# Two spatial gating layers: every projection from seven block products in place of eight

## The reference, cut to what matters

```python
def sgu_mixer(h, w_in, gain, w_s, b_s, w_out):
    u, v, z = jnp.split(h @ w_in, 3, axis=-1)          # 1024 -> 3 x 2048
    u = jax.nn.gelu(u)
    v = rms_norm_2(jax.nn.gelu(v), gain)
    vc = v.reshape(bsz, length // 128, 128, 8, 256)
    mixed = jnp.einsum('gpq,bcqgd->bcpgd', w_s, vc) + b_s.T[:, :, None]
    s = u * mixed.reshape(bsz, length, 2048)
    return (s * jax.nn.silu(z)) @ w_out                # 2048 -> 1024
```

## Time and profile before

| | |
|---|---|
| runs, median (lowest to highest) | 4984.64 us (4980.01 to 4988.49) |
| span of the profiled execution | 4981.9 us |
| TensorE busy | 4775.0 us, 96% |
| VectorE, ScalarE, GpSimd busy | 1474.1, 1080.2, 322.4 us |
| layer 0: v, u and z with mixing, out | from 1789.89, 1956.08 and 2311.37 us |
| layer 3: u and z with mixing, out | from 4623.95 and 4860.86 us |

### The profile page before, as it was taken

How to read it: one execution, slowest core, us unless ns; L and a number is a source line. 1 busy time by engine, 2 the same in 40 slices (tenths; PEclk the granted TensorE clock), 3 DMA queues, 4 the chain that set the end, 5 groups by cost and what they waited for, 6 DMA issues and landing times.

```text
span 4981.9 us, 62040 instructions
## 1 busy us (share of the span) xinstructions
PE 4775.0 (96%) x26926; PEld 2606.3 (52%) x26926; DVE 1474.1 (30%) x2789; ACT 1080.2 (22%) x2094; POOL 322.4 (6%) x302
## 2 busy tenths in 40 slices
PE   8999999999999999999999988988999999999999
PEld 4444444444444444665545557776544555644443
DVE  3621110363111010000044337785301443410100
ACT  1131000113100022110033124443211333311210
POOL 1100000110000000000003200000000101000000
PEclk9999999998999999999999999999999999999999
DMA  3151212115122211111134332322111000111211
GB/s 122 60 203 68 76 67 77 70 59 203 61 78 70 71 50 68 51 43 50 54 127 137 128 91 79 82 78 105 60 50 52 28 14 28 44 51 68 84 68 59
DMA packets 115069, 378.31 MB, mean 76 GB/s; under 512 B 32752, under 2 KB 58480, under 8 KB 85360
## 3 DMA queue, kind: packets, MB, share of 16 engines
q1 hardware_dynamic: 103840, 332.92, 19.2%
q0 software_dynamic: 9808, 37.75, 2.3%
q10 hardware_dynamic: 1152, 3.67, 0.2%
HBM read 334.46 MB, written 39.85 MB: 75 GB/s over the span
## 4 chain that ended last, share of the span: by engine, by line
PE 90%; DVE 6%; ACT 2%; issue 2%; DMA 0%; POOL 0%; POOLq 0%; DVEq 0%; ACTq 0%; SPq 0%
PE ps L522 43%; PE ps L334 21%; PE ps L543 7%; PE ps L3421 2%; PE ps L1782 2%; PE ps L340 2%; PE ps L3343 1%; PE ps L991 1%; PE ps L947 1%; PE ps L3432 1%; PE ps L2437 1%; PE ps L3346 1%; PE ps L3342 1%; PE ps L3344 1%; PE ps L450 0%
## 5 line engine op out<-in xcount | busy, mean ns | idle before, releaser
L522 PE MATMUL ps<-A,W 128*128 128x512 f32 (+1 forms) x5344 | 2149.8, 562 | 23.6 <-DVE A L494 8.8
L522 PEld LDWEIGHTS ps<-A,W 128*128 128x128 f32 x5344 | 1017.5, 192 | 1105.4 <-issue 1063.1
L334 PE MATMUL ps<-A,W 64*64 64x64 f32 (+3 forms) x3264 | 661.7, 380 | 10.1 <-ACT A L3586 5.8
L334 PEld LDWEIGHTS ps<-A,W 128*128 128x128 f32 (+2 forms) x3264 | 349.8, 163 | 305.8 <-issue 282.1
L334 PEld LDWEIGHTS ps<-A 64*64 64x64 f32 (+2 forms) x8416 | 401.1, 147 | 150.1 <-issue 94.9
L334 PE MATMUL ps<-A 64*64 64x64 f32 (+3 forms) x8416 | 438.2, 237 | 42.9 <-ACT A L2653 14.1
L543 PE MATMUL ps<-W,A 128*128 128x512 f32 (+1 forms) x896 | 366.0, 570 | 1.8 <-ACT A L1568 1.8
L543 PEld LDWEIGHTS ps<-W,A 128*128 128x128 f32 x896 | 172.0, 193 | 191.1 <-issue 183.8
L436 ACT ACTIVATE A<-R 128x512 f32<-128x512 f32 (+1 forms) x96 | 52.6, 574 | 759.3 <-DVE R L1578 330.5
L1698 DVE SCALAR_TENSOR_TENSOR A<-ps,V,A 128x512 f32<-128x512 f32 (+1 forms) x48 | 31.0, 661 | 486.9 <-PE ps L334 486.3
L1578 DVE SCALAR_TENSOR_TENSOR R<-ps,MOD,R 128x512 f32<-128x512 f32 (+1 forms) x48 | 31.7, 662 | 416.7 <-PE ps L522 410.6
(11 more groups left out here) (360 smaller groups left out, 4202.8 us busy)
## 6 DMA issues: line engine op xcount, KB each, us to landing
W<-in_ada SPq DMA_DIRECT2D x48, 1024.0 KB, 5.4
W<-in_w_up SPq DMA_DIRECT2D x44, 1024.0 KB, 4.8
W<-in_w_down SPq DMA_DIRECT2D x32, 704.0 KB, 4.1
W<-in_w_in SPq DMA_DIRECT2D x18, 1024.0 KB, 4.8
W<-in_sgu_v SPq DMA_DIRECT2D x16, 1024.0 KB, 4.9
W<-in_sgu_u SPq DMA_DIRECT2D x16, 1024.0 KB, 4.8
W<-in_sgu_z SPq DMA_DIRECT2D x16, 1024.0 KB, 4.8
W<-in_sgu_o SPq DMA_DIRECT2D x16, 1024.0 KB, 4.8
```

Of the source, the lines that this page charges most:

```text
L334: r = e.matmul(out, a, b, start=start and i == 0, stop=stop and i == len(pairs) - 1, skip_group_check=loose)
L522: t = e.matmul(ps, w[:, k, c:c + mc], x(k, seg), start=k == 0, stop=k == kt - 1)
```

## The change

Each product of the layer is cut into 2 by 2 blocks. With A the left (stationary) and B the right (moving) operand, `seven_pe` computes

- 1: A11 B11, 2: A12 B21
- 5: (A21+A22)(B12-B11), 6: (A21+A22-A11)(B22-B12+B11), 7: (A11-A21)(B22-B12)
- 3: (A12-A21-A22+A11) B22, 4: A22 (B21-B22+B12-B11)

in the order 1, 5, 6, 7, 2, 3, 4, into four banks A, C, B, D. Product 2 is added to the bank of 1, once ScalarE (in out: VectorE) has copied product 1 away; 3 is added to the bank of 5, and 4 to that of 7, once VectorE has read them. VectorE makes q = 1 + 6, q + 5 + 7, q + 5 + 3 and q + 7 + 4 (`joined_dve`).

The blocks: v in pairs of token tiles (3 in layer 0, 2 in layer 3), 256 columns a matmul, 4 matmuls a product; u and z per group over half of the tokens, 384 or 256 columns, 4 matmuls a product; out per pair of output blocks, 384 or 256 columns, 8 matmuls a product. Each set of seven needs four sums of the weights and four of the tokens. GpSimd makes those of the stationary side and of the v columns (`weights_pool`, `tokens` and `columns` in `sgu_pool`), VectorE those of the moving tokens (`differences`). The weight sums have one buffer, so each waits for the product of the set before that read it.

```diff
+def seven_pe(pl, e, at, left, right, kt, n, ring, ready, kept_, slabs_):
...
+    into(a, 1, left.b11, right.b11, True).then_inc(*made.next((at, 1)))
...
+    into(c, 5, left.s1, right.t1, True).then_inc(*made.next((at, 5)))
...
+    e.wait_ge(*kept_)
+    into(a, 2, left.b12, right.b21, False).then_inc(*made.next((at, 2)))
...
+    e.wait_ge(*S_.joined.at(at, "v"))
+    into(c, 3, left.s4, right.b22, False).then_inc(*made.next((at, 3)))
...
+    e.wait_ge(*S_.joined.at(at, 22))
+    into(d, 4, left.b22, right.t4, False).then_inc(*made.next((at, 4)))
...
+def weights_pool(pl, e, at, before, w, arrived):
...
+        e.wait_ge(*S_.seventh.at(before, 5))
+    e.tensor_tensor(w.all_s1, w.all21, w.all22, ALU.add).then_inc(*made.next((at, 5)))
...
+def joined_dve(pl, e, at, n, x, q, c12, c21, c22):
...
+    e.tensor_tensor(q, x, b, ALU.add).then_inc(*made.next((at, "q"), frees=(at, "B")))
+    e.wait_ge(*made.at(at, "q"))
+    e.tensor_tensor(c22, q, c, ALU.add).then_inc(*made.next((at, "v")))
...
 def sgu_pe(pl, e, b):
...
-                  ready=(lambda k, a: S_.modulated.at(i, k, a)) if c == 0 else None)
...
-    e.wait_ge(*S_.sgu_out.at(i, 7))
-    features_pe(pl, e, ("sgu_o", i), [("sgu_o", j, m) for m in range(8)], 16, P,
...
+            if p == 0 and k == 7 and q == 1:
+                events.append(S_.sgu_out.at(i, 7))
...
+    next(todo[0])
+    next(todo[1])
...
 def sgu_act(pl, e, b):
...
+        if a == 1:
+            kept_act(pl, e, ("sgu_u", i, 0), b.half, b.xt)
...
 def sgu_dve(pl, e, b):
...
     modulated_dve(pl, e, i, b.x, segs, b.before)
+    e.wait_ge(*S_.modulated.at(i))
+    later = differences("mod", b.corners, b.t)
+    next(later)
...
+    for _ in later:
+        pass
     e.wait_ge(*S_.v_squares.at(i))
...
     for g in range(8):
+        for name, dst in (("sgu_u", b.uu), ("sgu_z", b.zz)):
+            for _ in joined_dve(pl, e, (name, i, g), b.half, b.xt, b.qt, dst[:, 0, hi], dst[:, 1, lo], dst[:, 1, hi]):
+                pass
...
 def sgu_pool(pl, e, b):
...
+    columns(0)
+    for p in range(b.T // 2):
+        tokens(p)
+    for c in range(1, 4):
+        columns(c)
...
     for g in range(8):
+        for at in names[2 * g + 1:2 * g + 3]:
+            weights(at)
+            before = at
         e.wait_ge(*S_.sgu_u.at(i, g))
         e.wait_ge(*S_.sgu_z.at(i, g))
         e.tensor_tensor(b.uu, b.uu, b.zz, ALU.mult).then_inc(*S_.sgu_gated.next((i, g)))
+    e.wait_ge(*S_.seventh.at(before, 4))
...
+        weights_pool(pl, e, at, before, sgu_out_blocks(pl, b, p), [landed(pl, ("sgu_o", j, 2 * p + m)) for m in range(2)])
```

More of the change, by code:

```diff
@@ L344, in rows_of @@
     return lambda s: x[:, s[0]:s[0] + s[1]]
[L350 to L367, removed]
@@ L370, in rms_act @@
[L370 to L386, removed]
@@ L389, in rms_dve @@
[L389 to L392, removed]
-        e.wait_ge(*event)
[L394 to L409, removed]
+QUARTER = S // 2
@@ new lines, in seven_pe, with into, released @@
+def seven_pe(pl, e, at, left, right, kt, n, ring, ready, kept_, slabs_):
+    S_ = pl.S
+    made = S_.seventh
+    a, c, b, d = (at, "A"), (at, "C"), (at, "B"), (at, "D")
+    def into(key, p, x, y, first):
+        ps = bank(pl, key)[:, 0:n]
+        for k in range(kt):
+            for event in ready(p, k):
+                e.wait_ge(*event)
+            t = e.matmul(ps, x(k), y(k), start=first and k == 0, stop=k == kt - 1, skip_group_check=True)
+        return t
+    def released(p):
+        for key in slabs_.get(p, ()):
+            pl.slab_freed[key] = made.last()
+    take(pl, a, ring)
+    e.wait_ge(*free(pl, a))
+    into(a, 1, left.b11, right.b11, True).then_inc(*made.next((at, 1)))
+    released(1)
+    yield
+    take(pl, c, ring)
+    e.wait_ge(*free(pl, c))
+    into(c, 5, left.s1, right.t1, True).then_inc(*made.next((at, 5)))
+    released(5)
+    yield
+    take(pl, b, ring)
+    e.wait_ge(*free(pl, b))
+    into(b, 6, left.s2, right.t2, True).then_inc(*made.next((at, 6)))
+    released(6)
+    yield
+    take(pl, d, ring)
+    e.wait_ge(*free(pl, d))
+    into(d, 7, left.s3, right.t3, True).then_inc(*made.next((at, 7)))
+    released(7)
+    yield
+    e.wait_ge(*kept_)
+    into(a, 2, left.b12, right.b21, False).then_inc(*made.next((at, 2)))
+    released(2)
+    yield
+    e.wait_ge(*S_.joined.at(at, "v"))
+    into(c, 3, left.s4, right.b22, False).then_inc(*made.next((at, 3)))
+    released(3)
+    yield
+    e.wait_ge(*S_.joined.at(at, 22))
+    into(d, 4, left.b22, right.t4, False).then_inc(*made.next((at, 4)))
+    released(4)
+    yield
@@ L483, in spread_pe, with normed_dve @@
         t.then_inc(*S_.squares_summed.next(("rs", key, seg[0])))
-def normed_dve(pl, e, key, segs, out, gain):
+def normed_dve(pl, e, key, segs, out, gain, behind=None):
     S_ = pl.S
@@ new lines, in sgu_pe, with products, ready @@
+    for c in range(4):
+        begun = [values(c, p) for p in range(pairs)]
+        if c == 0 and pairs == 2:
+            for x in begun:
+                next(x)
+        for x in begun:
+            for _ in x:
+                pass
+    def products(at):
+        key = at[0], j, at[2]
+        def ready(q, k):
+            if k:
+                return []
+            events = [landed(pl, key)] if q == 1 else []
+            if q in (5, 6, 7, 3):
+                events.append(S_.weights_summed.at(at, q))
+            if at == ("sgu_u", i, 0) and q in (5, 6, 7, 4):
+                events.append(S_.tokens_summed.at("mod", i, q))
+            return events
+        return seven_pe(pl, e, at, sgu_blocks(pl, b, at), b.right, 4, b.half, "01234567", ready, S_.first_kept.at(at),
+                        {4: [key]})
@@ L1619, in sgu_pe @@
     for g in range(8):
[L1620 to L1621 removed]
+        for name in ("sgu_u", "sgu_z"):
+            for _ in products((name, i, g)):
+                pass
         if g == 0:
```

314 lines of the change are left out of this document (275 added, 39 removed).

## The result

The changed kernel takes 4878.1 us (median of 4 runs, 4873.99 to 4880.89) beside 4986.57 us (4 runs, 4980.01 to 4989.31) for the kernel before: ratio 0.9783, 95% interval 0.9769 to 0.9797. The forecast was 4878. The profiled execution of the changed kernel took 4880.89 us, the slowest of its four, with a span of 4878.9. So the span fell by 4981.9 - 4878.9 = 103.0 us, where the sum of the prediction said 106.9.

What follows compares the result with a forecast made beforehand. TensorE, busy 96% of the span, was taken as the bound. Terms -134.4 + 23.5 + 4 - 0.2 + 0.2 (end of out) = -106.9 us, from 4984.6 to 4877.7, say 4878 us; range 4860 to 4904.

Steps and rivals of the forecast that it cites:

- TensorE's work, -134.4 us: v, u, z and out of layers 0 and 3: new instructions at 215.8 or 322.5 ns take 134.4 us off TensorE.
- Rival E: New instructions of 256 or 384 columns cost a fixed 20 ns more each: 76 us, 4954 us; chance 0.05.
- Inside the loops, nothing: Sets of v, u, z and out: other products hide the new sums, so they cost nothing.
- Rival D: Sums out of PSUM late in every set; 1.8 us a set uses up the gain; 5118 us; chance 0.03.
- v to u, +23.5 us: First u: product 3 waits for sums queued behind v's scaling, 11.4 and 8.7 us, plus 3.4 of clock: +23.5 us.
- Start of v, +4 us: First products of v wait for token sums and differences: 3 us in layer 0, 1 us in layer 3, together +4.
- Start of out, 9.4 us forecast: Out: s waits for GpSimd's weight sum; 3.9 us in layer 0, 5.5 in layer 3; -0.2 against the old wait.
- the announced sign, s starting 2.3 us late: Start of out: s starts 2.3 us late, right behind L426 on GpSimd; if it starts at once, rival B.
- rival B: Starts of out and v: VectorE and GpSimd ports are not contended, 10 us more gain, 4868 us; chance 0.22.
- Rival C: Seams: the clock falls at each of six stops and stays low longer, 4892 us; chance 0.2.
- one clock loss a stop: Stops of TensorE at the seams: half clock for some 4 us behind a wait, 1.7 us lost each time.

Runs made afterwards that it cites:

- experiment 5: Changed kernel with product 3 issued right behind product 6 in every set, ahead of 7 and 2: 4989.05 us, ratio 1.0003 to the kernel before.
- experiment 1: Changed kernel with GpSimd's weight sums of out waiting for VectorE's last s: 4877.39 us (one run).
- experiment 2: Changed kernel with the first sums of u made ahead of the scaling of v: 4864.5 us, ratio 0.9753 to the kernel before.
- experiment 3: Changed kernel with the first two token differences of v behind the joins of its first pair: 4870.47 us (one run).
- experiment 7: Changed kernel with v of both layers back to eight block products: 4901.32 us, ratio 0.9831 to the kernel before.
- experiment 4: Changed kernel with s before weight sums, u's first sums before v's scaling, and v's first differences behind joins: 4851.82 us, ratio 0.9728 to the kernel before.
- experiment 6: Changed kernel with out of both layers back to eight block products and the old order of waits: 4916.25 us, ratio 0.9862 to the kernel before.

## Why the prediction was right

- **TensorE's work, -134.4 us.** Right: 322.5 ns at 384 columns, 216 at 256 (1948.94 to 1954.10; 1811.46 to 1813.19 is 8 in 1.73 us). Rival E is refuted by the same rows.
- **Inside the loops, nothing.** Right: gapless groups of 38.80 us. That a cover works here, and isn't merely unneeded, only experiment 5 shows. Rival D needed it gone.
- **v to u, +23.5 us.** Product 3 started 1970.45 - 1946.37 = 24.1 us behind the first u instruction in layer 0 and 4565.55 - 4548.16 = 17.4 in layer 3, forecast 24.3 and 17.4. The clock cost 4.08 - 2.58 = 1.5 us in layer 0 (forecast 1.7), and in layer 3 3.58 - 1.73 = 1.8 in product 3 and 4.31 - 3.46 = 0.9 in the two behind it, 2.7 (forecast 1.7). Idle time and clock together: 11.02 + 7.66 + 1.5 + 2.7 = 22.9 us. From start to start the loss is 41.2 - 28.6 = 12.6 us in layer 0 and 26.4 - 14.9 = 11.5 in layer 3, 24.1.
- **Start of v, +4 us.** In layer 0 2.08 + 0.65 us (forecast 3), in layer 3 1.29 + 0.24 (forecast 1). By the stages 3.5 and 1.5.
- **Start of out, 9.4 us forecast, about 6.8 measured.** The term that was off. Its mechanism stood: s was held up by one weight sum, landed 9.15 and 7.16 us behind the end of the last z (forecast 9.3 and 7.4), and experiment 1 removes it. Two sizes were not right. In layer 0 the clock kept full speed behind a stop of 1.84 us (windows above), where 1.7 us of loss was put in; it did so in the traces of experiments 2, 3, 5 and 7 too, but behind a stop of 1.92 us elsewhere it fell (last section), so no run shows what decides it. A difference and a weight sum in turn took 5.4 us, where 3.5 + 2.35 was put in, and product 7 was in time in layer 0. In layer 3 the waits add up to 0.89 + 1.12 + 0.29 + 0.66 + 0.66 + 0.90 = 4.5 us against 5.5. And the announced sign, s starting 2.3 us late, was the wrong form: it starts at once and lasts longer. By that sign of the prediction rival B would have been called right, though the blocking was there.
- **Rival B**, ports not contended, is refuted (3.82 us against 1.76). **Rival C**, clock falls at six stops, is refuted for this trace: it fell at two.
- **Outside.** The span fell by 4 us less than the touched stages: +6.6 us ahead of layer 0, where the code is unchanged and the granted clock in the first 100 us was 0.93 against 0.95, and -2.4 between the layers. Both lie inside what the same code does from one execution to the next (experiments); why it does is open. That the median hit 4878 so closely is partly luck: the interval of the ratio is 14 us wide, 2.6 us of gain more at out and these 4 us of loss are of opposite sign, and the stages' own misses (+0.5, -0.5, -2.1, +0.5, +1.1 and +0.1 us) nearly cancel.

The Trainium skill, page SBUF — State Buffer, section Who interferes with whom, says that a VectorE instruction with two SBUF inputs contends with a GpSimd instruction that reads SBUF, while one with at most one SBUF input, outside the two-port modes, does not. Both halves are now seen in this trace: s 3.82 in place of 1.76 us, L1964 with one operand in PSUM 0.55 us.

## What to carry to other kernels

When an algorithm trades matmul work for vector work, price the new sums at zero only if the product order puts other products between a sum and its reader: here that order is worth the whole 108 us gain. Then look for the seams, where a short sum that TensorE needs is queued behind a long operation that it doesn't (scaling of v, first differences): reordering these two, and putting s ahead of GpSimd's weight sums, gave another 26 us. And keep long two-operand SBUF work of VectorE and GpSimd apart where something critical starts.

## What was not expected of the hardware

- VectorE and GpSimd took whole instructions in turn where both had two SBUF operands: a VectorE TENSOR_TENSOR of 3072 elements takes 3.36 us ahead of GpSimd's and 5.38 to 5.50 behind it, GpSimd's of 1024 takes 5.46 in place of 2.34. The waiting doesn't show as idle time but inside the duration.
- TensorE's clock stood at 1.00 over 200 us with a stop of 1.30 us in every set. Behind a single stop its length alone doesn't tell what the clock does. It stayed at 1.00 behind 1.84 and 1.91 us (experiment 2), yet fell to 0.50 behind 1.92 us in experiment 4; it stayed at 1.00 behind 3.21 us at out of layer 3 in experiment 6, yet fell to 0.57 behind 2.73 us at the same place in the kernel before. Behind all stops of 3.44 us and more in the two gating layers it fell, in every trace. Experiment 4, then experiment 6, each with the window behind the stop:

```profile
1951.16 4.54 PE L365 MATMUL ps<-A 128*128 128x384 f32 x8 [1.92 <-DVE A L453]
1953.00:1955.00 2.00, 2.00 (x4) 1.01 (x3) 2.00 (x3) 0.44 (x1) 0.00 (x0) 0.50 0.62 248
...
4786.24 110.13 PE L574 MATMUL ps<-A,W 128*128 128x512 f32 x256 [3.21 <-DVE A L1903]
4786.00:4788.00 2.00, 1.76 (x4) 0.87 (x5) 0.19 (x1) 0.00 (x0) 0.00 (x0) 1.00 0.03 8
```

So a price of one clock loss a stop, as in the prediction, is a guess for stops of 2 to 3 us.
